# One level of Strassen's method in the up product of the second feed-forward of a two-block transformer kernel

## The reference

```python
D_FF = 4 * D_MODEL
...
def rms_norm(x, gain):
    xf = x.astype(jnp.float32)
    y = xf * lax.rsqrt(jnp.mean(xf * xf, axis=-1, keepdims=True) + NORM_EPS)
    return (y * gain.astype(jnp.float32)).astype(x.dtype)
...
        x = x + hybrid_mixer(h, lower_bounds[l], w_in[l], conv_w[l], conv_b[l], w_r[l], b_r[l],
                             w_i[l], b_i[l], lam[l], hg_norm[l], w_out[l])
        h = rms_norm(x, norm_mlp[l])
        x = x + jnp.square(jax.nn.relu(h @ w_up[l])) @ w_down[l]
    return rms_norm(x, norm_final)
```

## Time and profile before

| what | value |
|---|---|
| median of 3 runs | 3142.77 us (3142.29 to 3145.16) |
| the profiled execution, first to last instruction (span) | 3139.0 us |
| PE busy | 2962.1 us, 94% of the span |
| DVE, ACT, POOL busy | 1437.0, 598.6 and 1113.4 us |
| mean granted TensorE clock | 0.976 of full |

### The profile page before, as it was taken

How to read it: one execution, slowest core, us unless ns; L and a number is a source line. 1 busy time by engine, 2 the same in 40 slices (tenths; PEclk the granted TensorE clock), 3 DMA queues, 4 the chain that set the end, 5 groups by cost and what they waited for, 6 DMA issues and landing times. The chain is left out here.

```text
span 3139.0 us, 37276 instructions
## 1 busy us (share of the span) xinstructions
PE 2962.1 (94%) x14691; PEld 2460.7 (78%) x14691; DVE 1437.0 (46%) x1714; ACT 598.6 (19%) x719; POOL 1113.4 (35%) x474
## 2 busy tenths in 40 slices
PE   5999997999999999799999999999996999999998
PEld 4888886888888787687886888788785888888886
DVE  4224335344344444644454644545455344444445
ACT  3312313111111111423113112211312100010001
POOL 3232322334444334223322332333231544554442
PEclk9999998999999999899999999999997999999999
DMA  3111102111111111111111110111010211111111
GB/s 113 41 41 34 40 20 59 49 40 47 53 47 47 47 40 47 34 34 34 41 41 34 41 48 28 41 41 36 26 47 18 56 46 47 53 47 50 43 47 67
DMA packets 175602, 138.60 MB, mean 44 GB/s; under 512 B 4438, under 2 KB 163739, under 8 KB 175515
## 3 DMA queue, kind: packets, MB, share of 16 engines
q1 hardware_dynamic: 175515, 137.32, 14.6%
HBM read 133.11 MB, written 4.19 MB: 44 GB/s over the span
## 5 line engine op out<-in xcount | busy, mean ns | idle before, releaser
L139 POOL TENSOR_TENSOR w_hi<-w_raw,zero 128x1024 fp32r<-128x1024 f32 x210 | 429.4, 2045 | 1777.3 <-PE PB L150 580.0
L142 POOL TENSOR_TENSOR w_lo<-w_raw,w_hi 128x1024 fp32r<-128x1024 f32 x210 | 564.0, 2686 | 16.5
L148 PE MATMUL PA<-h_hi,w_hi 128*128 128x512 f32 x1120 | 445.5, 398 | 11.7 <-PEq L401 10.8
L150 PE MATMUL PA<-h_hi,w_lo 128*128 128x512 f32 x1120 | 438.5, 392 | 0.0
L149 PE MATMUL PA<-h_lo,w_hi 128*128 128x512 f32 x1120 | 438.5, 391 | 0.0
L353 DVE TENSOR_TENSOR X<-X,DD 128x512 f32<-128x512 f32 x344 | 233.0, 686 | 224.0 <-PE DD L150 223.9
L148 PE MATMUL PB<-h_hi,w_hi 128*128 128x512 f32 x816 | 320.8, 393 | 0.0
L150 PE MATMUL PB<-h_hi,w_lo 128*128 128x512 f32 x816 | 317.8, 390 | 0.0
L149 PE MATMUL PB<-h_lo,w_hi 128*128 128x512 f32 x816 | 317.5, 389 | 0.0
L148 PEld LDWEIGHTS PA<-h_hi,w_hi 128*128 128x128 f32 x1120 | 212.3, 190 | 57.4 <-issue 14.8
L150 PEld LDWEIGHTS PA<-h_hi,w_lo 128*128 128x128 f32 x1120 | 211.8, 189 | 45.1
(11 more groups left out here) (301 smaller groups left out, 5096.5 us busy)
## 6 DMA issues: line engine op xcount, KB each, us to landing
w_raw<-in_w_in SPq DMA_DIRECT2D x64, 512.0 KB, 4.0
w_raw<-in_ffn_w_up SPq DMA_DIRECT2D x44, 512.0 KB, 3.8
w_raw<-in_w_up SPq DMA_DIRECT2D x32, 512.0 KB, 4.1
w_raw<-in_w_down SPq DMA_DIRECT2D x32, 512.0 KB, 3.5
w_raw<-in_gla_w_in SPq DMA_DIRECT2D x24, 512.0 KB, 3.7
w_raw<-in_ffn_w_down SPq DMA_DIRECT2D x22, 512.0 KB, 3.5
X<-in_x SPq DMA_DIRECT2D x8, 512.0 KB, 6.6
w_raw<-in_gla_w_out SPq DMA_DIRECT2D x8, 512.0 KB, 3.7
```

Of the source, the lines that this page charges most:

```text
L139: pool.tensor_tensor(hi, raw, self.core.zero[:, 0:1].broadcast_to([P, UNIT]), ALU.add)\
L142: pool.tensor_tensor(lo, raw, hi.bitcast(F32), ALU.subtract).then_inc(self.split, 1)
L148: pe.matmul(out, ah, bh, start=first, stop=False)
L150: return pe.matmul(out, al, bh, start=False, stop=last)
```

## The change

The up product of a chunk, [256 hidden features by 1024 inner] by [1024 inner by 1024 rows], is cut into 2 by 2 blocks on both sides and formed with seven block products (P1 to P7, Winograd's form) in place of eight. A block product is 4 slices by 3 matmuls of 128x512. The sums of weight blocks are made by POOL for each chunk (`pair_low`); ACT makes the high parts of the weight blocks and POOL the low parts, in half slots of 512 elements (`Ring`), where POOL alone worked before. The sums of the input blocks (T1, T2, T3 and NT4) are made once, in the norm at the end of the hybrid mixer (`PairNorm`), for pairs of row tiles m and m+4 together. The block products meet in PSUM: two are accumulated on others, ACT keeps one (`keep`), and DVE forms five sums (`combine`). The down product has the same matmuls, ordered by column half first.

```diff
+class Ring:
...
+    def high(self, act, i, p, source, sem, value):
+        act.wait_ge(sem, value)
+        wait(act, self.used, self.free(i, p))
+        act.copy(self.slot(i, p)[0], source).then_inc(self.hi_done, 1)
...
+    def low(self, pool, i, p, source):
+        hi, lo = self.slot(i, p)
+        pool.wait_ge(self.hi_done, self.done(i, p))
+        pool.tensor_tensor(lo, source, hi.bitcast(F32), ALU.subtract).then_inc(self.split, 1)
...
+    def pair_low(self, pool, i, p, u, arrived, part):
+        a11, a12, a21, a22 = (self.block(x) for x in ("P1", "P2", "P7", "P4"))
+        at = {x: p + n for n, x in enumerate(PRODUCTS)}
+        if part == 0:
+            pool.wait_ge(self.raw_in[0], 16 * arrived[0])
+            pool.wait_ge(self.raw_in[1], 16 * arrived[1])
+            wait(pool, self.summed, 4 * u)
+            pool.tensor_tensor(self.S, a21, a22, ALU.add).then_inc(self.summed, 1)
+            self.low(pool, i, at["P1"], a11)
+            pool.wait_ge(self.summed, 4 * u + 1)
+            pool.tensor_tensor(a21, a11, a21, ALU.subtract).then_inc(self.summed, 1)
+            self.low(pool, i, at["P5"], self.S)
+            return
+        pool.wait_ge(self.split, self.done(i, at["P5"]))
+        pool.tensor_tensor(self.S, self.S, a11, ALU.subtract).then_inc(self.summed, 1)
+        self.low(pool, i, at["P7"], a21)
+        self.low(pool, i, at["P6"], self.S)
+        self.low(pool, i, at["P2"], a12)
+        pool.wait_ge(self.split, self.done(i, at["P2"]))
+        pool.wait_ge(self.summed, 4 * u + 3)
+        pool.tensor_tensor(a12, a12, self.S, ALU.subtract).then_inc(self.summed, 1)
+        self.low(pool, i, at["P4"], a22)
+        self.low(pool, i, at["P3"], a12)
...
+def pair_product(pe, core, ring, i, p, n):
+    name = PRODUCTS[n]
+    bank = {"P1": core.PA[:, 0:HALF], "P2": core.PA[:, 0:HALF], "P5": core.PA[:, HALF:SEQ], "P3": core.PA[:, HALF:SEQ],
+            "P7": core.PB[:, 0:HALF], "P4": core.PB[:, 0:HALF], "P6": core.PB[:, HALF:SEQ]}[name]
+    more = name in ("P2", "P3", "P4")
+    pe.wait_ge(ring.split, ring.done(i, p + n))
+    ah, al = (x.rearrange("p (k n) -> p k n", k=4) for x in ring.slot(i, p + n))
+    bh, bl = core.right[RIGHT[name]]
+    for k in range(4):
+        pe.matmul(bank, ah[:, k, :], bh[:, k, :], start=(k == 0 and not more), stop=False, skip_group_check=more)
+        pe.matmul(bank, ah[:, k, :], bl[:, k, :], start=False, stop=False, skip_group_check=more)
+        mm = pe.matmul(bank, al[:, k, :], bh[:, k, :], start=False, stop=(k == 3), skip_group_check=more)
+    mm.then_inc(ring.used, 1)
...
+    def scalar(self, act):
...
+                act.wait_ge(self.vars, k)
+                act.activation(c.sd[:, k - 1:k], c.ms[:, k - 1:k], ACT.Sqrt).then_inc(self.roots, 1)
+            q, odd = (k - 5) // 2, (k - 5) % 2
+            if 0 <= q < 4 and not odd:
+                act.wait_ge(self.turned, 2 * q + 2)
+                wait(act, self.lo_b, q)
+                act.copy(self.Z[:, 0:2, :], c.PB.rearrange("p (b s) -> p b s", b=2)).then_inc(self.kept, 1)
+                act.copy(self.out(0, 2, q)[0], c.PA.rearrange("p (b s) -> p b s", s=P)).then_inc(self.hi, 1)
+            elif 0 <= q < 4:
+                act.wait_ge(self.t2, q + 1)
+                act.copy(self.out(2, 2, q)[0], self.temp(3, 2)).then_inc(self.hi_t, 1)
+                act.wait_ge(self.t3, q + 1)
+                act.wait_ge(self.nt4, q + 1)
+                act.copy(self.out(4, 3, q)[0], self.temp(0, 3)).then_inc(self.hi_b, 1)
...
+    def vector(self, dve, arrive):
...
+                    .then_inc(self.vars, 1)
+            q, odd = (k - 5) // 2, (k - 5) % 2
+            if 0 <= q < 4 and odd:
+                dve.wait_ge(self.t2, q + 1)
+                dve.wait_ge(self.t3, q + 1)
+                dve.tensor_tensor(self.Z[:, 2, :], c.PA[:, HALF:SEQ], self.Z[:, 4, :], ALU.subtract)\
+                   .then_inc(self.nt4, 1)
+            m = k - 2
+            if 0 <= m < MT:
+                dve.wait_ge(self.roots, m + 1)
+                dve.reciprocal(c.rs[:, m:m + 1], c.sd[:, m:m + 1])
+                if m == 0:
+                    dve.wait_ge(self.row_in, 16)
+                wait(dve, self.turned, m - 1)
+                dve.drain()
+                dve.scalar_tensor_tensor(out=self.xn[:, m % 2, :], in0=c.X[:, self.ORDER[m], :],
+                                         scalar=c.rs[:, m:m + 1], in1=self.row, op0=ALU.mult, op1=ALU.mult)\
+                   .then_inc(self.scaled, 1)
+            if 1 <= q < 5 and not odd:
+                dve.wait_ge(self.hi_b, q)
+                dve.tensor_tensor(self.out(4, 3, q - 1)[1], self.temp(0, 3), self.out(4, 3, q - 1)[0].bitcast(F32),
+                                  ALU.subtract).then_inc(self.lo_b, 1)
+            if 0 <= q < 4 and not odd:
+                dve.wait_ge(self.kept, q + 1)
+                dve.wait_ge(self.hi, q + 1)
+                wait(dve, self.lo_t, q)
+                dve.tensor_tensor(self.Z[:, 3, :], self.Z[:, 0, :], c.PA[:, 0:HALF], ALU.subtract)\
+                   .then_inc(self.t1, 1)
+                dve.tensor_tensor(self.out(0, 2, q)[1], c.PA.rearrange("p (b s) -> p b s", s=P),
+                                  self.out(0, 2, q)[0].bitcast(F32), ALU.subtract).then_inc(self.lo, 1)
...
+    def gpsimd(self, pool):
+        for q in range(4):
+            pool.wait_ge(self.t1, q + 1)
+            pool.tensor_tensor(self.Z[:, 4, :], self.Z[:, 1, :], self.Z[:, 3, :], ALU.subtract).then_inc(self.t2, 1)
+            pool.tensor_tensor(self.Z[:, 0, :], self.Z[:, 1, :], self.Z[:, 0, :], ALU.subtract).then_inc(self.t3, 1)
+            pool.wait_ge(self.hi_t, q + 1)
+            pool.tensor_tensor(self.out(2, 2, q)[1], self.temp(3, 2), self.out(2, 2, q)[0].bitcast(F32),
+                               ALU.subtract).then_inc(self.lo_t, 1)
...
+    def tensor(self, pe, arrive):
...
+            q = (k - 4) // 2
+            if q < 0 or k % 2:
+                continue
+            for t in (2 * q, 2 * q + 1):
+                pe.wait_ge(self.scaled, t + 1)
+                if t % 2 == 0:
+                    wait(pe, self.lo, q)
+                    wait(pe, self.nt4, q)
+                else:
+                    wait(pe, self.kept, q)
+                pair = (c.PA, c.PB)[t % 2]
+                for j in range(KT):
+                    mm = pe.transpose(pair[:, j * P:(j + 1) * P], self.xn[:, t % 2, j * P:(j + 1) * P], c.ident)
...
+    def square_ffn(self, name, ring, W_up, W_down, rows):
...
+                def up(i):
+                    sp.wait_ge(ring.split, first_of(i))
+                    for n in range(2):
+                        sp.dma_start(c.raw[:, n, :].rearrange("p (k n) -> p k n", k=KT),
+                                     WU[:, :, ds(i * (2 * P) + n * P, P)]).then_inc(ring.raw_in[n], 16)
+                def down(i, h):
+                    if isinstance(i, int) and i == chunks:
+                        sp.wait_ge(ring.split, first_of(i) + 2 * h)
+                    else:
+                        sp.wait_ge(ring.split, ring.done(i, (5, D0 + 1)[h]))
+                    sp.dma_start(c.raw[:, 1, :].rearrange("p (k n) -> p k n", k=2),
+                                 WD[:, ds((i - 1) * 2, 2), h * HALF:(h + 1) * HALF]).then_inc(ring.raw_in[1], 16)
...
+            def _(pe):
+                def up(i):
+                    gate = {"P1": (s["prod"], i * 2 - 1), "P7": (s["prod"], i * 2), "P2": (s["kept"], i + 1),
+                            "P4": (s["u3"], i + 1), "P3": (s["c22"], i + 1)}
+                    for n, product_name in enumerate(PRODUCTS):
+                        if product_name in gate:
+                            wait(pe, *gate[product_name])
+                        pair_product(pe, c, ring, i, 0, n)
...
+                with pe.Fori(1, chunks) as i:
+                    up(i)
+                    pe.wait_ge(s["a_lo"], i * 2)
+                    for h in range(2):
+                        pe.wait_ge(ring.split, ring.done(i, down_at(i, h) + 1))
+                        for m in range(MT):
+                            mm = tile(i, m, h, MT * h + m)
+                            mm.then_inc(*((s["down_mm"], 1) if m < MT - 1 else (ring.used, 2)))
...
+                def keep(i):
+                    act.wait_ge(ring.used, ring.done(i, 0))
+                    wait(act, s["a_lo"], i * 2 - 1)
+                    act.copy(u2, X1).then_inc(s["kept"], 1)
+                def relu(i):
+                    act.wait_ge(s["c12"], i + 1)
+                    for t, pair in enumerate((c.PA, c.PB)):
+                        act.activation(U[t], pair, ACT.Relu).then_inc(s["relu"], 1)
+                def a_high(i, prior):
+                    act.wait_ge(ring.used, prior)
+                    for k in range(2):
+                        act.wait_ge(s["prod"], i * 2 + (k + 1))
+                        act.copy(ahi[k], U[k]).then_inc(s["a_hi"], 1)
...
+                with act.Fori(1, chunks) as i:
```

(84 more changed lines are left out.)

211 lines of the change are left out of this document (201 added, 10 removed).

## The result

The changed kernel takes 3154.47 us (median of 5 runs, 3152.38 to 3156.53) beside 3142.29 us for the kernel before: a ratio of 1.0039, 95% interval 1.0026 to 1.0051. It is slower by 12.2 us, where 7 us less were forecast.

The account below looks back on a forecast made before the run. PE was taken to bound f2, busy throughout at full clock. Fewer matmuls -43.5, hand-over +28.3, gap +4.7, slow clock +2.0, end +1.2 sum to -7.3 us: median from 3142.8 to 3135.5, say 3136 us, range 3129 to 3148.

Parts of the forecast that it names:

- a chunk should take 180 x 0.2267 = 40.8 us, with added cost 0: In f2, PE stays the bound in each chunk, 180 matmuls at 0.2267 us, other engines' work hidden.
- The walk of the queues: One chunk of the new code followed in order through the engines' queues; tightest slacks 1.1 and 1.5 us, on DVE.
- The hand-over: From the hybrid's last down product to f2's first matmul, through the norm: 67.8 against 39.4 us, +28.3 us.
- The gap between chunks 0 and 1: In f2, P1 of chunk 1 waits for P3 of chunk 0 with no down product between: +4.7 us.
- the slow matmuls behind it: PE at slow clock after the gap between chunks 0 and 1: +2.0 us.
- The end: End of f2: the last weight half stands behind ACT's copies and DVE's second low part: +1.2 us, bounds 0 and 2.
- The sum: Whole kernel: -43.5 + 28.3 + 4.7 + 2.0 + 1.2 = -7.3 us.
- f2 with seam and end: Stage f2: the saving of -43.5 with +4.7 gap, +2.0 slow clock and +1.2 at the end; forecast 35.6 us shorter.
- what 12 matmuls a chunk cost: f2's up product falls from 96 to 84 matmuls a chunk; 16 chunks by 12 by 0.2267 us = -43.5 us.
- The case that adding to an old bank slows the matmuls: Rival in f2: a 4.7 us gap recurs per chunk, +70 us, or accumulation on an old bank slows matmuls; chance 0.04.
- DVE late behind P3: Rival in each f2 chunk: relus late, third add misses its slack; +1 to +11 us, 3144 to 3154; chance 0.10.

Follow-up runs that it names:

- the aligned kernel: The changed kernel with one small table moved behind `c.free`, so block operands and activations start at multiples of 128 bytes; 3134.17 us, ratio 0.9974.
- a2_only_T: The aligned kernel with 64 unused bytes behind the block operands, so the activations alone start 64 bytes off; 3145.42 us, ratio 1.0006.
- b3_h_off64: The kernel before with the normalized rows (h_hi, h_lo) 64 bytes beside a multiple of 128; 3183.32 us, ratio 1.0130.

## Why the prediction was wrong, point by point

- **The step that failed** is "so a chunk should take 180 x 0.2267 = 40.8 us, with added cost 0". The walk of the queues was right: PE waits nowhere in a chunk. The price of a matmul was carried over from operands at multiples of 128 to ones 64 bytes beside; 132 of the 180 have such an operand. It cost 41.63 - 40.80 = 0.83 us a chunk (0.67 for the 96 with the stationary operand off, 0.16 for the rest), 692.7 - 679.3 = 13.4 us in f2. Why the address counts, no run tells. I had read from the diff where the tiles lie in order, but worked out no address.
- **The hybrid** was not in the sum: +2.6 us for its activations at the same kind of address, and -3.4 us for the split that no longer stands beside DVE's scaling. The diff shows the removed call; which DVE instruction it had held was in the trace before.
- **The hand-over** (forecast +28.3, 69.1 us in all) was +30.0, 70.8 us, in the order forecast and with POOL last. POOL's 512 elements took 1.27 us, not 1.2. (The prediction's own 67.8 - 39.4 is 28.4, not 28.3.)
- **The gap between chunks 0 and 1** (forecast 4.7) was 4.62 us; the slow matmuls behind it cost 2.9 us, not 2.0. Busy time by stretch of the aligned kernel behind its gap (PE starts again at 2479.77), in the columns of the earlier trace rows:

```profile
2480.00:2485.00 5.00, 5.00 (x12) 3.95 (x13) 2.35 (x2) 3.86 (x6) 4.92 (x4) 0.50 0.02 3
2487.00:2492.00 5.00, 5.00 (x24) 4.12 (x23) 0.00 (x0) 0.62 (x1) 4.84 (x5) 1.00 0.00 0
```

  Granted clock 0.50 (1.2 GHz) with 12 matmuls in 5 us, then 1.00 (2.4 GHz) with 24 (the ones that reach into a stretch count). The first fourteen matmuls take 6.1 us, 0.43 apart behind the first, for 14 x 0.2267 = 3.2. This price isn't fixed: in the trace of a2_only_T only the first seven are slow behind the same gap of 4.6 us, and it is 1.4 us.
- **The end** (forecast +1.2): PE's last wait is 4.70 us against 3.53, +1.2.
- **The sum, with its price mended:** the aligned kernel takes 3134.2 us beside 3142.6, 8.4 us less, for a forecast of 7.3 us less; its f2 with seam and end is 34.1 us shorter, forecast 35.6. So block products do bring what 12 matmuls a chunk cost, and the hand-over takes 30 of it back. That 8.4 stands so near 7.3 is luck in part: the hand-over cost 1.9 us more than forecast and f2 gave 1.5 less, and the 3.7 us of the hybrid's tail, which weren't in the sum, make up for both.
- **All differences together:** by the table the profiled execution of the changed kernel is 12.9 us longer than that of the kernel before: +7.0 up to the seventh split, -3.4, +30.0 and -20.7. The forecast had 0, 0, +28.3 and -35.6.
- **The rivals.** The case that adding to an old bank slows the matmuls had named the right symptom (slower matmuls) and the wrong cause; the case had a chance of 0.04, priced at a wait of 4.7 us a chunk. DVE late behind P3 didn't occur. No rival had the operands' addresses.

## What to carry to other kernels

When a change moves buffers, work out the start address of every matmul operand before pricing a matmul; a round-up to 32 bytes is enough to lose up to 3% on each. Where a stage's period is off and its engine has no waits, compare the pitch of one instruction with that of before, then move the buffers alone. Before extra work goes into POOL's idle time, look at what DVE does there: here the work made DVE's instructions longer, and 1.4 to 2.3 of the 4.6 us went back.

## What the runs showed of the hardware

- A 128x512 matmul (fp32r) at full clock takes 0.2267 us start to start with both operands at multiples of 128 bytes in the partition and 0.2333 us when the stationary one is 64 or 32 bytes off, or in b3_h_off64 the moving one 64. The profile's median duration of one goes from 389 ns to between 394 and 398 (stationary) or to 394 (moving), and the engine counts as busy all the same. Other distances, both operands off together and other types were not run.
- The 256-column matmuls of b3_h_off64, whose stationary rows were 64 bytes off, didn't grow: their medians were 279 to 280 ns beside 283, and from start to start 118 ns beside 120.
- In the changed kernel's chunk, P6 took 2.77 us and P2 2.72, though the operands of both are aligned, and P7, P4 and P3, whose moving operands are off, 2.76, 2.76 and 2.75, where 12 x 0.2333 would be 2.80. In the kernel with aligned block operands all five took 2.72. No run tells why.
